# Seven block products in place of eight for 18 of the 22 gate and up tile pairs of each feed-forward stage

## The reference, cut to what matters

```
def rms_norm(x, g):
    y = x * lax.rsqrt(jnp.mean(x * x, axis=-1, keepdims=True) + EPS)
    return y * g

def swiglu(h, w_gate, w_up, w_down):
    return (jax.nn.silu(h @ w_gate) * (h @ w_up)) @ w_down

h = h + 0.5 * swiglu(rms_norm(h, norms[i, 0]), ffn_w_gate[i, 0], ffn_w_up[i, 0], ffn_w_down[i, 0])
...
h = h + 0.5 * swiglu(rms_norm(h, norms[i, 2]), ffn_w_gate[i, 1], ffn_w_up[i, 1], ffn_w_down[i, 1])
```

## Time and profile before

| | |
|---|---|
| runs, median of 3 | 1941.94 us (1941.71 to 1943.26) |
| profiled execution, from the first to the last instruction | 1941.1 us |
| PE busy | 1912.9 us, 99% |
| DVE / ACT / POOL busy | 1031.1 / 635.9 / 287.6 us |
| granted TensorE clock, mean | 0.997 |
| the up halves of the first two feed-forward stages, first matmul to first matmul of the down half | 7.5 to 251.0 and 489.8 to 730.7 us |

### The profile page before, as it was taken

The page is one execution under the profiler, slowest core; times in us unless marked ns, Lnnn a source line. Parts: engine busy times, 40 slices in busy tenths (PEclk is TensorE's granted clock), DMA queues, the critical chain, the costliest instruction groups (busy, mean ns, idle before and its releaser), DMA issues.

```text
span 1941.1 us, 24220 instructions
## 1 busy us (share of the span) xinstructions
PE 1912.9 (99%) x8970; PEld 1543.5 (80%) x8970; DVE 1031.1 (53%) x1506; ACT 635.9 (33%) x959; POOL 287.6 (15%) x219
## 2 busy tenths in 40 slices
PE   8999999999999999999999999999989999999998
PEld 6888888777888888887888888877658888888886
DVE  5444477674644442347545442279984644442345
ACT  5323222245332222224323222234563333222222
POOL 2000001212300000224000000163243200000225
PEclk9999999999999999999999999999999999999999
DMA  4323323232223332322322332231101323322321
GB/s 175 107 86 102 104 93 109 76 101 92 87 87 106 99 97 98 109 76 94 109 90 88 109 104 92 97 113 66 55 1 44 109 86 106 99 97 98 109 76 54
DMA packets 56730, 179.59 MB, mean 93 GB/s; under 512 B 12144, under 2 KB 12144, under 8 KB 56656
## 3 DMA queue, kind: packets, MB, share of 16 engines
q1 hardware_dynamic: 54656, 173.69, 27.5%
q0 software_dynamic: 928, 3.02, 0.5%
q10 hardware_dynamic: 1088, 2.10, 0.3%
HBM read 175.04 MB, written 3.15 MB: 92 GB/s over the span
## 4 chain that ended last, share of the span: by engine, by line
PE 91%; DVE 5%; ACT 2%; POOL 1%; issue 0%; DMA 0%; DVEq 0%; SPq 0%; POOLq 0%; ACTq 0%
PE ps L1799 58%; PE ps L1817 26%; PE ps L2249 2%; PE ps L1912 1%; PE ps L2148 1%; DVE sm L1006 1%; POOL sumsq L1279 0%; ACT prob L1539 0%; PE ps L2167 0%; DVE work L982 0%; DVE stat L980 0%; PE ps L1963 0%; PE ps L1827 0%; PE ps L2198 0%; DVE rstd L398 0%
## 5 line engine op out<-in xcount | busy, mean ns | idle before, releaser
L1799 PE MATMUL ps<-x_hi,w_hi 128*128 128x512 f32 x1728 | 681.1, 394 | 8.6 <-ACT w_hi L356 7.5
L1799 PE MATMUL ps<-x_hi,w_lo 128*128 128x512 f32 x1728 | 673.8, 390 | 0.0
L1799 PE MATMUL ps<-x_lo,w_hi 128*128 128x512 f32 x1728 | 673.5, 390 | 0.0
L364 DVE TENSOR_TENSOR w_lo<-raw,w_hi 128x1024 fp32r<-128x1024 f32 x310 | 398.4, 1301 | 407.9 <-ACT w_hi L356 403.1
L356 ACT ACTIVATE w_hi<-raw 128x1024 fp32r<-128x1024 f32 x322 | 332.3, 1050 | 337.7 <-PE ps L1817 293.6
L1799 PEld LDWEIGHTS ps<-x_hi,w_hi 128*128 128x128 f32 x1728 | 325.1, 188 | 82.0 <-ACT w_hi L356 7.5
L1799 PEld LDWEIGHTS ps<-x_lo,w_hi 128*128 128x128 f32 x1728 | 325.0, 188 | 68.5 <-issue 2.4
L1799 PEld LDWEIGHTS ps<-x_hi,w_lo 128*128 128x128 f32 x1728 | 324.8, 188 | 68.7 <-DVE w_lo L364 0.8
L1817 PE MATMUL ps<-act_hi,w_hi 128*128 (+1 forms) x720 | 280.3, 389 | 0.0
L1817 PE MATMUL ps<-act_hi,w_lo 128*128 (+1 forms) x720 | 280.1, 389 | 0.0
L1817 PE MATMUL ps<-act_lo,w_hi 128*128 (+1 forms) x720 | 280.1, 389 | 0.0
(11 more groups left out here) (361 smaller groups left out, 1323.0 us busy)
## 6 DMA issues: line engine op xcount, KB each, us to landing
raw<-in_weights SPq DMA_DIRECT2D x322, 512.0 KB, 3.3
h<-in_xT ACTq DMA_DIRECT2D x4, 512.0 KB, 6.7
out<-result SPq DMA_DIRECT2D x4, 512.0 KB, 3.0
p_raw<-in_pT POOLq DMA_DIRECT2D x2, 512.0 KB, 4.2
scratch_u<-u_sc SPq DMA_DIRECT2D x1, 512.0 KB, 6.7
u_grp<-scratch_u SPq DMA_DIRECT2D x1, 512.0 KB, 4.2
scratch_y<-y_grp SPq DMA_DIRECT2D x2, 256.0 KB, 3.1
y_ch<-scratch_y SPq DMA_DIRECT2D x1, 512.0 KB, 3.6
```

Of the source, the lines that this page charges most:

```text
L364: dve.tensor_tensor(w_lo[:, slot], raw[:, slot], w_hi[:, slot].bitcast(F32), SUB)\
L1799: last = pe.matmul(ps[:, bank], w[:, slot, k], x[:, k], start=(k == 0 and part == 0), stop=(k == KD - 1 and part == 2))
```

## The change

Pairs 0 to 3 of each stage stay as they were (`PLAIN = 4`). For pairs 4 to 21 the work of a pair is seen as a product of 2 x 2 blocks: two outputs (gate, up), two halves of the 1024 channels (upper and lower four tiles), two halves of the 512 tokens. Eight block products become seven, after Winograd's form of Strassen's scheme. A block product is 4 blocks x 3 = 12 matmuls of 128 x 256, so a pair has 84 matmuls of 256 columns in place of 48 of 512.

For that, sums of weights are needed in each pair (`weight_sums`: one DVE operation of 1024 elements a partition and two of 512), and their own hi and lo parts (`sums_hi`, `sums_lo`). The block products share partial sums: ACT copies four partial results of 128 x 256 from PSUM to `part_sum` (`copy_part`), and DVE adds them to what PSUM holds (`gate_left`, `up_right`, `up_left`). The sums of the residual need the true normed residual, since rstd differs between the two token halves. So ACT writes h times gain to `xn` (`gained`, eight operations of 128 x 512), POOL multiplies by rstd (`normalised`, two operations of 128 x 2048), DVE makes four sums (`residual_sums`, 128 x 1024 each), and ACT and DVE split seven quarters into hi and lo (`residual_hi`, `residual_lo`, 128 x 1024 each). rstd is then no longer multiplied in on the way out. The product stays in float32 in `act_f`; its hi and lo parts are made while group 0 of the down half runs (`act_high`, `act_low`).

First DVE, with the block that prepares a stage's first fast pair:

```diff
+        def halves_of(first, b):
+            turn = 2 * (first % SLOTS)
+            t2 = (turn + 4) % (2 * SLOTS)
...
+            def weight_sums(i, b):
+                slot = slot_of(first, 2 * b)
+                own = raw_half[:, 2 * slot:2 * slot + 4]
...
+                dve.tensor_tensor(w_sum[:, 0:2], own[:, 0:4:3],
+                                  own[:, 2].unsqueeze(1).to_broadcast([P, 2, T]), ADD)\
+                   .then_inc(fast["w_sums"], 1)
+                dve.wait_ge(fast["w_sums"], counted(3, f, i, b, 1))
+                dve.tensor_tensor(w_sum[:, 2], w_sum[:, 0], own[:, 3], ADD)\
+                   .then_inc(fast["w_sums"], 1)
+                dve.wait_ge(fast["w_sums"], counted(3, f, i, b, 2))
+                dve.tensor_tensor(w_sum[:, 3], w_sum[:, 2], own[:, 1], ADD)\
+                   .then_inc(fast["w_sums"], 1)
...
+            def fast_tile(i, b, more=True, down=False):
+                if more:
+                    weight_sums(i, b + 1)
+                    sums_lo(i, b + 1, 0)
+                gate_left(i, b)
+                if more:
+                    own_lo(i, b + 1, 0)
...
+                up_right(i, b)
+                if more:
+                    sums_lo(i, b + 1, 1)
+                    own_lo(i, b + 1, 1)
...
+                up_left(i, b)
+                product(i, b)
 
             two_tiles(0, peeled=True)
-            with dve.Fori(1, NF // 2, 1) as i:
-                two_tiles(i)
+            split_lo(dve, first, 6)
+            split_lo(dve, first, 7)
+            weight_sums(2, 0)
+            residual_sums()
+            for o in range(4):
+                residual_lo(o)
+            own_lo(2, 0, 0)
+            gate(1, 0)
+            up(1, 0)
+            sums_lo(2, 0, 1)
+            gate(1, 1)
+            low(1, 0)
+            sums_lo(2, 0, 0)
+            for o in range(4, 7):
+                residual_lo(o)
+            up(1, 1)
+            own_lo(2, 0, 1)
+            low(1, 1)
+            with dve.Fori(PLAIN // 2, NF // 2 - 1, 1) as i:
+                fast_tile(i, 0)
+                fast_tile(i, 1)
```

On ACT, `gained` stands ahead of `root`, and a pair is this:

```diff
+            def gained():
+                if n == 0:
+                    act.wait_ge(sum_step, KD - 1)
+                for k in range(KD):
+                    act.activation(xn[:, k], h[:, k], ACT.Copy, scale=gains[:, n, k:k + 1])\
+                       .then_inc(fast["x_gained"], 1)
...
+            def fast_tile(i, b, more=True, down=False):
+                copy_part(i, b, 0)
+                copy_part(i, b, 1)
+                copy_part(i, b, 2)
+                if more:
+                    sums_hi(i, b + 1, 0)
+                    own_hi(i, b + 1, 0)
...
+                copy_part(i, b, 3)
+                if more:
+                    sums_hi(i, b + 1, 1)
...
+                silu_left(i, b)
+                if more:
+                    own_hi(i, b + 1, 1)
+                silu_right(i, b)
```

On PE a block product, and on POOL the normed residual:

```diff
+            def product(bank, at, hi, lo, start, stop, done):
+                for k in range(KH):
+                    cols = slice(k * P, (k + 1) * P)
+                    for part, (w, x) in enumerate(((wf_hi, hi), (wf_hi, lo), (wf_lo, hi))):
+                        last = pe.matmul(ps[:, bank, 0:HALF], w[:, at, cols], x[:, k],
...
+                last.then_inc(done, 1)
...
+        def normalised(pool, f, n):
+            pool.wait_ge(rstd_ready, n + 1)
+            for half in range(2):
+                rows = slice(KH * half, KH * half + KH)
+                pool.wait_ge(fast["x_gained"], KD * f + KH * half + KH)
+                pool.tensor_tensor(xn[:, rows], xn[:, rows],
+                                   rstd[:].unsqueeze(1).to_broadcast([P, KH, T]), MULT)\
+                    .then_inc(fast["x_normed"], 1)
```

More of the change, by code:

```diff
@@ new lines, in ffn_up_dve, with down_dve, act_low @@
+            own_lo(2, 0, 1)
[3 more added lines that the diff above has]
+                fast_tile(i, 1)
+            fast_tile(NF // 2 - 1, 0)
+            fast_tile(NF // 2 - 1, 1, more=False, down=True)
+        def down_dve(dve, n, first, steps, q, scale, after=None, early={}, beside=(), split=0, f=None):
+            def act_low(t):
+                s = ffn_sems
+                dve.wait_ge(s["act_hi_ready"], t + 1 + NF * f)
+                span = slice(t * T, (t + 1) * T)
+                dve.tensor_tensor(act_lo[:, span], act_f[:, span], act_hi[:, span].bitcast(F32), SUB)\
+                   .then_inc(s["act_ready"], 1)
@@ L457, in low @@
                     gained_lo(dve, n, k)
[L459 to L466, removed]
+            for j in range(split, steps):
                 split_lo(dve, first, AHEAD + j)
+                if f is not None:
+                    for t in range(PLAIN + 2 * j, min(PLAIN + 2 * j + 2, NF)):
+                        act_low(t)
                 if j in early:
@@ L1428, in two_tiles @@
                 if peeled:
+                    gained()
                     root(act, n)
@@ new lines, in ffn_up_act, with down_act, act_high @@
+            fast_tile(NF // 2 - 1, 0)
+            fast_tile(NF // 2 - 1, 1, more=False, down=True)
+        def down_act(act, n, first, steps, after=None, at=AFTER, split=0, early={}, then=None, f=None):
+            def act_high(t):
+                s = ffn_sems
+                span = slice(t * T, (t + 1) * T)
+                act.wait_ge(s["prod_done"], t + 1 + NF * f)
+                if t >= 6:
+                    act.wait_ge(chunk_used, first - 1)
+                act.activation(act_hi[:, span], act_f[:, span], ACT.Copy).then_inc(s["act_hi_ready"], 1)
+            for j in range(split, steps):
@@ L1453, in down_act @@
                 split_hi(act, first, AHEAD + j)
+                if f is not None:
+                    for t in range(PLAIN + 2 * j, min(PLAIN + 2 * j + 2, NF)):
+                        act_high(t)
                 if j in early:
@@ L1841, in ffn_up_pe @@
                     squares(pe, n)
[L1842 to L1847, removed]
+            def product(bank, at, hi, lo, start, stop, done):
[3 more added lines that the diff above has]
+                        last = pe.matmul(ps[:, bank, 0:HALF], w[:, at, cols], x[:, k],
+                                         start=(start and k == 0 and part == 0),
+                                         stop=(stop and k == KH - 1 and part == 2),
+                                         skip_group_check=True)
+                last.then_inc(done, 1)
```

250 lines of the change are left out of this document (216 added, 34 removed).

## The result

The changed kernel takes 1956.06 us (median of 4 runs, 1955.59 to 1956.27), the kernel before 1942.25 on the same chip: a ratio of 1.0071, 95% interval 1.0056 to 1.0086. It is .7% slower, where the prediction had 1920, a gain. The measured time lies near the upper end of the stated range (1898 to 1958), which was put there for a rival, with the likeliest case on the other side of the kernel before. The profiled span grew from 1941.1 to 1954.2 us.

The account below looks back on a forecast made before the run. PE's up-half matmuls bound the kernel before; DVE would barely bind the fast pairs. The span 1941.1 less 81.4 for the loop plus 59 for the starts gave 1918.7, .8 more for the median: 1920 us, range 1898 to 1958.

Parts of the forecast that it names:

- the likeliest case: Whole kernel: DVE-bound at 9.6 to 9.9 us a fast pair, 53 to 65 us of starts, 1908 to 1932; chance .45.
- The pace of the short matmul: PE in fast pairs: a 256-column matmul every .113 us, so 9.52 us a pair, held at odds of some 3 to 2.
- the two bounds: PE's 256-column matmul: .1133 us if the excess goes with columns, .120 if with the instruction; 9.52 or 10.08 a pair.
- exactly 32 cycles: PE at full clock: argument that the 13.4 ns excess is paid per instruction, given for the slower case of chance .33.
- The starts: Preparing the first fast pair in each stage: 12.5 us for each of three stages, 21 for the first, 59 together.
- DVE loses about 2.5 us of the 12 in which POOL works: Second stage's start: DVE slowed beside POOL's two long multiplies, two splits taking 4.29 us against 2.36 in the loop.
- the 2.5 us for P3: Stage start: PE waits another 2.5 us or so before the third block product, for ACT's queued copy of the first.
- The loop on DVE: Fast pairs: DVE needs 9.75 us a pair, above PE's 9.52, so it binds; 72 pairs gain 81.4 us.
- The rival of a longer loop: Fast pairs: DVE's and ACT's loop takes 10.6 us a pair through cross waits and queued copies, giving 1980; chance .12.
- The order of `gained`: First stage: ACT's eight copies ahead of the root make it 5.0 us late, and PE waits 5.0 at chunk 4.
- The down half and the moved low parts: Down half: DVE's 2.4 and ACT's 2.3 us a chunk hide under PE's 5.44; counted 0, at most 2.
- The rival that came true: Fast pairs: the 13.4 ns belong to each matmul, so PE needs 10.08 us a pair, about 1948 in all; chance .33.

Follow-up runs that it names:

- the best versions: Changed kernel with six plain pairs, eight short POOL operations, late first-stage copies and spread residual sums: 1911.04 us; also with the last plain up ahead of two residual quarters: 1910.12.

## Why the prediction was wrong

Against its own sum (1941.1 - 81.4 + 59 = 1918.7), the span of 1954.2 is 35.5 us too long. Two terms hold nearly all of it. (Against 1920, 1.1 us come from the step from span to median: .8 was added, and each run of the changed kernel lies 1.9 above its own span.)

- **The pace of the short matmul, 23.8 us.** The step that failed is "I take .113, since at half clock nothing is paid for each instruction". Of the two bounds, .1133 and .120, the upper one was measured to the last digit, in the changed kernel and by itself. The half clock, from which I argued, is no guide: the first fast matmuls after a stage's wait go at .213, 256 columns at 1.2 GHz with nothing on top, and the same form at full clock has its 13.4 ns. The excess "exactly 32 cycles, which looks like a cost per instruction" was in my hands and given the smaller chance. 72 x (10.08 - 9.75) = 23.8.
- **The starts, 11.1 us.** 70.1 measured, 59 forecast. The step: "DVE loses about 2.5 us of the 12 in which POOL works". I took the tax as a rate, from 512-element POOL operations in the earlier trace rows, where DVE's two splits lost 1.9; it is a wait for the end of the instruction that POOL has under way, and that was now four times as long. In the second stage DVE lost 6 us, its chain came 3.4 us later than forecast, and PE waited 1.6 for a split besides (3.7 for two splits in the third). Leaving POOL out gives back 24 us where I had booked 10. One other item was booked too high: the 2.5 us for P3 were not paid, as PE did not wait ahead of P3, with P1 and P2 at half clock before it.
- **The loop on DVE** was right: 9.65 measured with PE's load lightened, 9.75 forecast, the wait for ACT 1.12 against 1.07. It was not the bound, because PE's pace was .120. The rival of a longer loop (1980) falls.
- **The order of `gained`** in the first stage: 5.0 forecast, 4.55 us of PE's idle time there and 5.7 us when undone.
- **The down half and the moved low parts**: nothing forecast, and at most .6 us found outside the up halves (13.1 less 12.5).
- **The rival that came true**, .120 a matmul, was given .33 and 1948. Its own terms, 1941.9 - 54.7 + 60, come to 1947; with the measured 70.1 and 57.6 they come to 1954. So this rival had the right mechanism for the pace, and it too was short by the starts.

What stays open: why the 13.4 ns are there at full clock and not at half, and whether they belong to the matmul or to the hand-over from its weight load; no run separated these. Also open is about 1 us of the 7.6 that the first stage still pays in the best versions.

## What to carry to other kernels

A scheme that saves multiplications by cutting the blocks finer can pay a fixed price per matmul first: read it from a pace row at full clock (it is the distance between starts less columns over clock) and take it off before counting what the scheme saves. Here 12.5% fewer products were 7.4% of PE's time in the loop, and four starts of 15 to 22 us ate that; the same scheme, with 16 fast pairs in place of 18, won 32 us once POOL's operations were short, the copies in the first stage stood behind the root, and the preparation was laid where DVE waits anyway and had enough PE work as cover. A fixed cost at the start of each stage deserves as much of the sum as the loop.

## What the runs showed of the hardware

- A DVE operation with two SBUF inputs that meets a POOL multiply under way waits until its end: 7.83 us beside one of 8.98, 3.46 and 4.38 beside two of 4.62 and 5.59, 1.39 and 1.07 beside short ones. POOL waits for DVE in the same way (2.27 us in place of 1.3). DVE operations with a PSUM input beside them kept their .68.
- For the same elements POOL needs 8.98, 10.16 and 13.38 us in one, two and eight instructions. Most of the difference between two and eight is its waits for DVE: eight alone would be 10.1. Long POOL instructions are dearer for DVE when it comes second.
- Matmuls with 128 x 128 weights in this type start every .2267, .120 and .111 us for 512, 256 and 128 columns at full clock; at half clock .425 and .213 for 512 and 256. The 13.4 ns over the columns are there only at full clock, and 128 columns run into the weight load.
